# A two-layer streaming encoder on eight cores: when the last tile's norm is done, and where four modulation blocks are loaded

## The reference, cut to what matters

```python
def run_trunk(x, c, ...):
    for i in range(2):                     # layer 0: convolution module, layer 1: window attention
        mod = silu(c) @ w_mod[i] + b_mod[i]            # 6 * 2048 numbers for each sequence
        sh1, sc1, g1, sh2, sc2, g2 = split(mod, 6)
        h = rms_norm(x, norm_mix[i]) * (1 + sc1) + sh1
        y = conv_module(h) if i == 0 else attention(h)
        x = x + g1 * y
        h = rms_norm(x, norm_ffn[i]) * (1 + sc2) + sh2
        g, u = split(h @ w_gu[i], 2)                   # 2048 -> 2 * 5632
        x = x + g2 * ((silu(g) * u) @ w_down[i])       # 5632 -> 2048
    return rms_norm(x, norm_out), ...

def conv_module(h):                        # pw1: 2048 -> 4096, pw2: 2048 -> 2048
    a, gt = split(h @ w_pw1 + b_pw1, 2)
    z = depthwise_conv31(a * sigmoid(gt)) + b_dw
    return silu(layer_norm(z)) @ w_pw2 + b_pw2
```

## Time and profile before

| What | Value |
|---|---|
| Median of 3 runs | 3286.67 us |
| The profiled execution, its own time | 3290.7 us |
| Its span on the slowest core (core 1) | 3289.5 us |
| Spans of the eight cores | 3271.6 to 3289.5 us |
| PE busy | 3018.0 us, 92% |
| DVE busy | 1182.5 us, 36% |
| ACT busy | 674.9 us, 21% |
| POOL busy | 259.0 us, 8% |
| Granted clock of PE, mean over the core | 0.963 |

### The profile page before, as it was taken

The page is one execution under the profiler, slowest core; times in us unless marked ns, Lnnn a source line. Parts: engine busy times, 40 slices in busy tenths (PEclk is TensorE's granted clock), DMA queues, the critical chain, the costliest instruction groups (busy, mean ns, idle before and its releaser), DMA issues.

```text
span 3289.5 us, 55198 instructions; the slowest of 8 cores (3271.6 to 3289.5 us)
## 1 busy us (share of the span) xinstructions
PE 3018.0 (92%) x21834; PEld 1812.1 (55%) x21834; DVE 1182.5 (36%) x2585; ACT 674.9 (21%) x1413; POOL 259.0 (8%) x438
## 2 busy tenths in 40 slices
PE   1199998899899999999999889998999999999997
PEld 0055555445455555555555456666566666666664
DVE  0453335542143113141231749934222413131417
ACT  1132224332000000000001558833200000000012
POOL 0000001000000000000000113300000000000000
PEclk9599998999999999999999999989999999999999
DMA  9966766523767777777754222233243444444443
GB/s 193 195 114 123 140 130 139 131 52 71 135 128 124 134 128 128 129 128 126 126 95 65 43 58 60 55 59 71 52 77 58 84 77 78 71 71 77 78 73 111
DMA packets 78910, 327.74 MB, mean 100 GB/s; under 512 B 20849, under 2 KB 39921, under 8 KB 44465
## 3 DMA queue, kind: packets, MB, share of 16 engines
q0 software_dynamic: 41200, 283.66, 49.3%
q1 hardware_dynamic: 37458, 40.54, 4.2%
HBM read 593.07 MB, written 10.19 MB: 183 GB/s over the span
## 4 chain that ended last, share of the span: by engine, by line
PE 85%; DVE 6%; ACT 3%; DMA 2%; issue 2%; SPq 2%; another core or an unknown queue 1%; POOL 0%; DVEq 0%; ACTq 0%; POOLq 0%
PE ps L310 85%; SPq L305 2%; DVE SCR L316 1%; DMA X<-xT 1%; ACT SCR L313 1%; ACT HB L313 1%; DVE X L319 1%; DVE SCR L687 1%; DVE X L316 1%; DMA RING<-wgu 1%; DVE UBraw L1280 0%; POOL HB L699 0%; DMA kT_o<-UBraw 0%; ACT L313 0%
## 5 line engine op out<-in xcount | busy, mean ns | idle before, releaser
L310 PE MATMUL ps<-HB,RING 128*128 128x384 bf16 (+2 forms) x11712 | 1937.6, 326 | 71.0 <-ACT HB L313 22.2
L310 PEld LDWEIGHTS ps<-HB,RING 128*128 128x128 bf16 x11712 | 1142.3, 99 | 818.2 <-issue 122.0
L310 PE MATMUL ps<-UBraw,RING 128*128 128x384 bf16 (+3 forms) x5248 | 814.4, 313 | 1.9 <-ACT UBraw L313 0.7
L310 PEld LDWEIGHTS ps<-UBraw,RING 128*128 128x128 bf16 x5248 | 492.9, 98 | 302.0 <-issue 19.6
L319 DVE SCALAR_TENSOR_TENSOR X<-ps,MOD,X 128x16 f32<-128x16 f32 (+2 forms) x1120 | 453.9, 446 | 441.2 <-PE ps L310 438.4
L316 DVE TENSOR_TENSOR UBraw<-ps,SCR 128x384 bf16<-128x384 f32 (+2 forms) x264 | 144.2, 547 | 1188.3 <-PE ps L310 1182.1
L313 ACT ACTIVATE SCR<-ps 128x384 f32<-128x384 f32 (+4 forms) x314 | 155.5, 496 | 1785.2 <-PE ps L310 1762.6
L313 ACT ACTIVATE SCR<-X 128x384 bf16<-128x384 f32 (+3 forms) x224 | 135.8, 608 | 263.0 <-DVE X L319 260.6
L310 PE MATMUL ps<-SCR,ONESB 128*32 128x296 bf16 (+3 forms) x368 | 85.4, 336 | 87.1 <-ACT SCR L313 83.1
L128 POOL DMA_DIRECT2D RING<-wgu x88 | 46.8, 531 | 1172.7 <-PE ps L310 1172.6
L310 PE MATMUL ps<-RING,SCT 128*32 128x512 bf16 x768 | 60.5, 406 | 62.2 <-DMA RING<-wmod 35.1
(11 more groups left out here) (104 smaller groups left out, 1114.4 us busy)
## 6 DMA issues: line engine op xcount, KB each, us to landing
RING<-wmod POOLq DMA_DIRECT2D x96, 1024.0 KB, 14.1
RING<-wgu POOLq DMA_DIRECT2D x88, 1024.0 KB, 9.1
RING<-wdn POOLq DMA_DIRECT2D x40, 1024.0 KB, 9.4
RING<-wpw POOLq DMA_DIRECT2D x24, 1024.0 KB, 14.1
RING<-wqkv POOLq DMA_DIRECT2D x10, 1024.0 KB, 8.9
X<-xT SPq DMA_DIRECT2D x4, 2368.0 KB, 54.2
RING<-wo POOLq DMA_DIRECT2D x8, 1024.0 KB, 9.3
X<-xT SPq DMA_DIRECT2D x8, 768.0 KB, 4.5
```

What stands on the lines that cost most here:

```text
L310: return PE.emit(nc.tensor.matmul(out, lhsT=lhsT, rhs=rhs, start=start, stop=stop, **kw))
```

## The change

It has five parts. (1) Blocks 40 and 41 of layer 0's modulation move from `ffn` to pw2: they are planned after pw2_4 and pw2_5 and run in `proj_rest` behind the last item of these, in bank 7. The other six of that vector stay behind gu 2 to 7, also in bank 7. (2) In group 2 the modulation blocks between the four down blocks of group 1 are left out, and come later. (3) In pw1 the 24 blocks are dealt out to the chunks in another pattern, by which each vector ends with a chunk. (4) `norm_apply` has three buffers T1 instead of two and POOL takes c % 4 == 1; the sample columns of tile 2 are done between its first six chunks, in a work area of their own; `hb` holds a token for each chunk, and PE waits for chunk k ahead of its matmul k. SQ has seven buffers. (5) `proj_rest` flushes all squares at each item. The flush and finish of tile 2 move into a generator `last_tile`, which the next stage takes up: in `ffn` its first step comes between the gate and the up half of `gu(0,0)`, and six chunks each come ahead of the epilogues of `gu(0,1)` and `gu(1,0)`, the rest ahead of that of `gu(1,1)`; at k and v its first step comes behind the first `kv_group`.

```diff
@@ ffn_schedule @@
-    mods = [("mod", 0, 40 + b) for b in range(8)] if li == 0 else []
+    mods = [("mod", 0, 42 + b) for b in range(6)] if li == 0 else []
...
-    out += mods
-    mods = []
...
                 for b in range(4):
                     out.append(("dn", G - 1, b))
-                    if later:
+                    if later and G != 2:
                         out.append(later.pop(0))
@@ buffers @@
-        T1 = carve(SCR, 0, (128, 2, 416), F32)
-        SQ = [SQA[:, i, :] for i in range(4)] + [SQB[:, i, :] for i in range(4)]
+        T1 = carve(SCR, 0, (128, 3, 384), F32)
+        SQ = [SQA[:, i, :] for i in range(4)] + [SQB[:, i, :] for i in range(3)]
+        WS = carve(UBraw, 24000, (128, 2, KC, 16), F32)
@@ the plan of the ring @@
-            for _ in range(1 if c % 2 == 0 else 2):
+            for _ in range((2, 1, 2, 1, 2, 2, 1, 2, 1, 2, 2, 1, 1, 2, 1, 1)[c]):
...
             ring.add(f"pw2_{b}", wpw2[b], ALL)
+            if b in (4, 5):
+                ring.add(f"mod0_{36 + b}", wmod[36 + b], ALL)
@@ norm_apply @@
+            smp = sample_cols(nm) if t == 2 else iter(())
             for c in range(KC):
-                i = c % 2
+                i = c % 3
                 DVE.wait(t1free[i])
                 tt(cv3(T1[:, i, 0:n], lay, t), xv(c, lay, t, True), cv3(RSTD[:, t % 2, 0:n], lay, t), ALU.mult)
-                if c % 4 == 3:
+                tx = DVE.tick()
+                if c % 4 == 1:
...
-                yield
-            if t == 2:
-                DVE.wait(*t1free)
...
-            nm.hb[t] = (ACT.tick(), DVE.tick(), POOL.tick())
-            yield
+                nm.hb[t].append(t1free[i])
+                next(smp, None)
+                if c < KC - 1:
+                    yield
+            for _ in smp:
+                pass
+            nm.hb[t] = [(nm.smp, x) for x in nm.hb[t]]
+            rsfree[t % 2] = DVE.tick()
+            yield
+
+        def sample_cols(nm):
+            tk = [None, None]
+            for op in range(3):
+                for s in range(2):
+                    w = WS[:, s]
+                    DVE.wait(tk[s])
+                    if op == 0:
+                        tt(w, X[:, :, 1152 + 16 * s:1168 + 16 * s],
+                           RSTD[:, 0, 384 + 16 * s:400 + 16 * s].unsqueeze(1).to_broadcast([128, KC, 16]), ALU.mult)
+                    elif op == 1:
+                        tt(w, w, nm.A[:, :, 1 + s:2 + s].to_broadcast([128, KC, 16]), ALU.mult)
+                    else:
+                        tt(HB[:, :, 1184 + 16 * s:1200 + 16 * s], w, nm.SH[:, :, 1 + s:2 + s].to_broadcast([128, KC, 16]), ALU.add)
+                    tk[s] = nm.smp = DVE.tick()
+                    yield
+
+        def last_tile(nm):
+            norm_flush(nm, 0)
+            norm_finish(nm, 2)
+            yield
+            yield from nm.apply(nm, 2)
@@ proj_rest @@
-                norm_flush(nm, max(1, len(nm.pend) - 2))
+                if li == 0 and (b, h, t) in ((4, 1, 2), (5, 1, 2)):
+                    mod_block(0, 36 + b, 7)
+                norm_flush(nm, 0)
...
-                    norm_flush(nm, 0)
...
-            return gen
+            pump(gen, 40)
+            nm.war[2] = tp
+            return last_tile(nm)
@@ head of pw2, after each proj_group @@
+                norm_flush(nm1, len(nm1.pend) - 1)
@@ ffn @@
-                if j == 0:
-                    PE.wait(*nm_in.hb[t])
                 bank_wait(i)
                 for k in range(KC):
+                    if j == 0:
+                        PE.wait(*nm_in.hb[t][k])
                     mm(PS[i][:, 0:n], w[:, k, 0:128], hv(k, lay, t), k == 0, k == KC - 1)
                 tg = PE.tick()
+                if mid is not None:
+                    mid()
...
-            gu(0, 0, pm(6))
+            gu(0, 0, None, pm(1))
             gu(0, 1, pm(6))
-            gu(1, 0, pm(20))
-            gu(1, 1)
+            gu(1, 0, pm(6))
+            gu(1, 1, pm(40))
...
-                    mod_block(it[1], it[2], 4)
+                    mod_block(it[1], it[2], 4 if it[1] else 7)
...
-            norm_flush(nm, 0)
-            norm_finish(nm, 2)
-            return nm, nm.apply(nm, 2)
+            return nm, last_tile(nm)
@@ k and v @@
-            PE.wait(*nm2.hb[t])
             bank_wait(bi)
             for k in range(KC):
+                PE.wait(*nm2.hb[t][k])
...
-        pump(genN, 4)
         kv_group(0, 0, 0)
-        pump(genN, 4)
+        pump(genN, 2)
         kv_group(0, 1, 0)
-        pump(genN, 4)
+        pump(genN, 5)
         kv_group(1, 0, 0)
+        pump(genN, 5)
+        kv_group(1, 1, 0)
         pump(genN, 40)
-        kv_group(1, 1, 0)
```

More of the change, by code:

```diff
@@ L650, in __init__ @@
                 self.left = [KC] * 3
-                self.hb = [None] * 3
+                self.hb = [[] for _ in range(3)]
                 self.done = [None] * 3
+                self.smp = None
                 self.tok = None
                 self.war = [None] * 3
-        sqfree = [None] * 8
-        t1free = [None, None]
+        sqfree = [None] * 7
+        t1free = [None] * 3
         rsfree = [None, None]
@@ L662, in norm_sq @@
             n = CN[nm.lay][t]
-            i = nsq % 8
+            i = nsq % 7
             nsq += 1
@@ L702, in norm_apply @@
                 else:
-                    ACT.wait(DVE.tick())
+                    ACT.wait(tx)
                     act(hv(c, lay, t, True), cv3(T1[:, i, 0:n], lay, t), AF.Identity, scale=nm.A[:, c, 0:1], bias=nm.SH[:, c, 0:1])
                     t1free[i] = ACT.tick()
-                yield
-            if t == 2:
-                DVE.wait(*t1free)
-                for s in range(2):
-                    w = T1F[:, 256 * s:256 * s + 256].rearrange("p (c b) -> p c b", b=16)
-                    tt(w, X[:, :, 1152 + 16 * s:1168 + 16 * s],
-                       RSTD[:, 0, 384 + 16 * s:400 + 16 * s].unsqueeze(1).to_broadcast([128, KC, 16]), ALU.mult)
-                for s in range(2):
-                    w = T1F[:, 256 * s:256 * s + 256].rearrange("p (c b) -> p c b", b=16)
-                    sync(DVE)
-                    tt(w, w, nm.A[:, :, 1 + s:2 + s].to_broadcast([128, KC, 16]), ALU.mult)
-                for s in range(2):
-                    w = T1F[:, 256 * s:256 * s + 256].rearrange("p (c b) -> p c b", b=16)
-                    sync(DVE)
-                    tt(HB[:, :, 1184 + 16 * s:1200 + 16 * s], w, nm.SH[:, :, 1 + s:2 + s].to_broadcast([128, KC, 16]), ALU.add)
-                t1free[0] = t1free[1] = DVE.tick()
@@ L880, in build_nc @@
         nm1 = Norm(0, [5, 6, 4], A1, MOD[:, 0, 48:64, :])
+        nm1.apply = norm_apply
         HEADB = [0, 1, 2, 3, 4, 7]
@@ L991, in ffn @@
             pm = lambda k: (lambda: pump(gen_in, k))
-            gu(0, 0, pm(6))
+            gu(0, 0, None, pm(1))
             gu(0, 1, pm(6))
-            gu(1, 0, pm(20))
-            gu(1, 1)
-            assert nm_in.hb[2] is not None
+            gu(1, 0, pm(6))
+            gu(1, 1, pm(40))
             ring.release(f"gu{li}_0", gu(0, 2))
@@ L1227, in build_nc @@
         t_gb = make_g1b(1, "bo")
-        POOL.wait(t_gb, *nm2.hb[2])
+        POOL.wait(t_gb, *nm2.hb[2][KC - 1], *nm2.hb[2][KC - 2])
         def x_bias(c):
```

16 lines of the change are left out of this document (7 added, 9 removed).

## The result

| | before | after |
|---|---|---|
| median of the runs | 3286.84 us (4 runs) | 3250.28 us (4 runs) |
| lowest run | 3283.93 us | 3244.2 us |
| profiled execution | 3290.7 us | 3249.67 us |
| span of the profiled slowest core | 3289.5 us (core 1) | 3248.6 us (core 7) |

The ratio is 0.9884, with a 95% interval of 0.9869 to 0.9898. The change gains 1.2%, less than the 2% bound. The forecast was 3239 us, 11 us faster than what came; the range, 3222 to 3261, holds it.

A forecast was written before the change was run, and what follows sets the result against it. PE, busy 3018.0 of 3289.5 us, was taken as the bound, leaving idle and low-clock time to win. Loads 24.3 and seams 11.7, 11.0 and 1.2 sum to 48.2 off 3290.7, giving a median of 3239 us, range 3222 to 3261.

The forecast's parts named there:

- vector's end in pw1: In pw1, PE's wait for DVE's transposes at a vector's first block and the slow work behind it go: 6.5 us.
- group 0: At the end of group 0, PE's wait of 8.77 and the slow product behind it go: 10.1 us.
- group 2: Behind the half-size down blocks, PE's wait of 4.76 and the slow product behind it go: 7.7 us.
- seam behind pw2: From pw2 to ffn, gu(0,2) starts earlier with the norm's faster pace: gain 11.7 us, bounds 5 and 21.0.
- seam behind wo: From wo to ffn, the same chain with less cover on PE: gain 11.0 us, bounds 4 and 22.1.
- k and v: Seam to k and v: the wait for the last square goes, 3.7 us stay; gain 1.2, bounds -3 and 4.9.
- Rival C: A load is late elsewhere: pairs of full chunks in pw1 and pw2 miss, four waits of 4 us; 3255 us, chance 0.09.
- Rival A: At the seams, buffers don't help: the pace stays at 0.815 us a chunk; 3253 us, chance 0.12.
- the charge of 2.4 for clock: In the seam from pw2 to ffn, one product slowed behind a wait, 7.72 instead of 5.4: 2.4 us off the gain.
- Rival B: In the norm, DVE and POOL exclude each other: four chunks take 2.70, 2.3 us more a seam; 3244 us, chance 0.13.
- Rival D: No wait stays at the seams, which gain 21.0, 22.1 and 4.9 us: 3215 us, chance 0.07.
- Rival E: Slower: 144 waits by chunk inside accumulation groups cost PE 0.5 us each, +72 us; 3311 us, chance 0.05.

The follow-up runs named there:

- one behind chunk 0: The changed kernel with one modulation block of pw1 behind chunk 0 instead of two, each vector still ending with a chunk: 3238.36 us, ratio 0.9835.
- pattern alone: The kernel before with only the change's pattern of modulation blocks in pw1: 3298.31 us, ratio 1.0015.
- reverse experiments: Blocks 40 and 41 put back at the end of group 0: 3249.87 us; separately, modulation blocks put back between group 1's half-size down blocks: 3248.21 us.
- repeated run: The changed kernel itself, unaltered, run again on another chip: 3255.28 us, ratio 0.9882 to the kernel before.

## Why the prediction was right or wrong

| term | forecast | in the changed kernel | by itself |
|---|---|---|---|
| vector's end in pw1 | 6.5 | 3.6 | 6.2 (one behind chunk 0) |
| group 0 | 10.1 | with group 2: 15.7 | 12.2 less some 1.2 of the blocks |
| group 2 | 7.7 | | 5.4 |
| seam behind pw2 | 11.7 | 15.7 | |
| seam behind wo | 11.0 | 13.0 | |
| k and v | 1.2 | 1.2 | |
| first convolution | nothing | -10.0 on the mean, -16.7 on core 7 | -9.0 (pattern alone) |
| other stretches | nothing | 0.8 | |
| sum | 48.2 | 40.0 | |

**The time** was missed by 11 us because of one step: "each vector now ends with a chunk" was costed for the weight loads that a chunk of 22.1 us must cover (20.1, which holds: no load is late in pw1 on any core), and not for SP's copies that land behind them. Of the queues that the moved block meets I counted POOL's and left SP's out. The step cost 10.0 in the first stretch and another 2.4 in the next, whose convolutions then run partly at the lower clock; that is also why pw1 gave 3.6 and not 6.2. Rival C had the right kind (a transfer late in pw1, 3255) with the wrong object and place. The trace of before would have shown it: its copies behind chunk 0 land 12.9 to 14.7 us after issue with two loads beside them, and behind chunk 1, with three loads, 19.9 to 20.8; and the first convolution leaves only 15.7. That alone gives a wait of 4 to 5 us, the size of what three of the eight cores showed (3.1, 3.9 and 4.2).

**Luck.** That 11 us were missed and not some 15 is because errors cancelled: the seams gave 6.0 more than forecast, the loads only 2.1 less. And the range reached up to 3261 for rivals A and C, not for this wait.

**The loads.** Group 0 and group 2 together were forecast at 17.8; the reverse experiments give 12.2 and 5.4, 17.6 together, but 1.2 of that is the blocks' own time, which the move only puts elsewhere. Group 2 was mis-sized, because I took the rows of one core. Its wait and the slow product behind it, 4.76 and 2.9 on core 1, were 3.8 and 1.25 on the mean of the eight cores (a product of 17.44), 5.0 together for 7.7; with group 0 mended and group 2 as before they are 3.6 and 1.7. The same means for group 0 are 8.9 and 2.05, 10.9 together for 10.1. The stretch as a whole got 15.7 shorter, some 2 us less than the reverse experiments add up to; 0.9 of these lie in `gu(0,2)` and `gu(1,2)`, the first two products behind the seam (12.1 for 11.3), and come back with tile 2 flushed early or waited for whole. So the shorter seam hands part of its lateness on to the products behind it.

**The seams** were under-forecast by 4.0 and 2.0. The walk behind pw2 itself held almost to the instruction. With its times moved by the 7.3 us by which pw2 ends later here: reciprocal done at 748.3 (measured 748.28), gate half done at 735.0 (735.2), flush over at 738.9 (739.1), `gu(0,2)` at 761.2 (759.8). The walk's end was 1.4 too late, and the charge of 2.4 for clock stood on top of it. That charge is what failed most. Before, three products of the seam took 5.1 us more than at full clock (7.72, 6.74 and 12.22 for 5.4, 5.4 and 10.8); now 80 matmuls take 14.31 for 13.5 and the next 45 7.82 for 7.6: 1.0 in all. The wait for a bank was 1.19 instead of 2.5, and nothing stood ahead of `gu(1,0)`. The 2.5 held a slip: a product of 5.4 behind a wait of 1.0 from 740.5 on ends at 746.9 and not at 746.0, so the walk gives 1.6. I took the pace at 0.60; it was 2.51/4 = 0.63. What gave the 2.0 behind wo I did not look into.

**The parts of the seam**, each by taking it back: three buffers 4.0 and 4.0, samples between the chunks 4.0 and 2.2, waits by chunk 3.5 and 1.8, squares flushed at once 3.3 and 0.7, the place of tile 2's flush +1.3 and -1.4. They don't add: each is measured with the others there.

**Rival B** (DVE and POOL exclude each other) was put at 2.70 for four chunks; 2.51 was measured. But the exclusion is there. POOL's piece takes 0.70 alone, and 1.21 on the mean where two of DVE's products lie beside it (160 pieces on the eight cores). DVE is held too: of 400 of its products beside a piece of POOL, 9 of 50 on each core, 72 took 0.74 to 0.90, where none of the 624 others took more than 0.56. The Trainium skill, "SBUF — State Buffer", section "Who interferes with whom", has the second to issue blocked while the first runs. The trace agrees: the 72 products all began 0.26 us or more behind POOL's piece. What B had wrong is who pays: in the walk of tile 1 DVE keeps its 0.51 a product, and POOL's piece is the one that gets longer. It comes back to DVE as the wait for POOL's buffer, 0.47 in four chunks: 4 x 0.51 + 0.47 = 2.51. Taking POOL out changed the seams by 0.2 and 0.6 to the slower side, with ACT setting the pace instead, so it doesn't price this.

**Rival D** needed seams with no wait; waits of 2.9, 1.2 and 0.6 remain. **Rival E** is false: 16 matmuls behind 16 waits took 2.76 us, and 0.33 us a wait would have been needed. **Rival A** is false by the experiment with two buffers.

**Why 16 us and not 4.** Copies behind chunk 0 with three loads landed after 18 to 20 us on three cores of the profiled run, after 23.5 on one and after 29 to 32 on four; in the repeated run, after 18.2 to 19.0 on four cores and 28.8 to 30.3 on the other four. POOL issues chunk 1's two loads 17.5 us behind chunk 0's three (183.83 and 201.37 on core 7). The packets that the DMA engines moved show the rest. The loads are 128 packets of 8 KB each, and the copies, with one small transfer issued behind them, 720 packets of some 0.6 KB. While both wait, the packets go one for one: 542 of the loads and 556 of SP's between 191.5 and 215.5 on core 7. So the copies, which have more packets than three loads, are not done before the loads beside them are. When chunk 1's loads were issued, the three loads had moved 3.05 of their 3.15 MB on core 0, and 2.36 on core 7. These are the packets, MB and share of the engines in the 4 us after that issue, core 0 (193.21 to 197.21) first, then core 7 (201.37 to 205.37); q0 has the loads and q1 SP's transfers:

```profile
q0 software_dynamic: 68, 0.43, 83.5%
q1 hardware_dynamic: 407, 0.18, 16.4%
```

```profile
q0 software_dynamic: 82, 0.67, 94.5%
q1 hardware_dynamic: 82, 0.04, 5.2%
```

On core 0 the loads ran out and the copies finished; on core 7 the two further loads joined before that, and up to the landing of the copies 639 packets of loads went by, which is all five loads. On core 0 it was 398, little more than three.

What stays open is why the later cores are fed more slowly. In every pair of neighbours (0 and 1, 2 and 3, ...), in the profiled run, the repeated one and the one with the pattern alone, it was the core that began pw1 earlier, by its own time, that had the shorter wait. On core 7 the DMA engines moved 111 and 162 GB/s in the first two stretches of 8 us from 183.5, against 152 and 213 on core 0 from 175.4, both with their engines nearly full in the second. The Trainium skill, "HBM Reference", section "Specifications (TRN2)", says that the two cores of a domain share its bandwidth; the trace fits that, but no run here separates the cores of a pair, and none holds back chunk 1's loads.

## What to carry to other kernels

When a plan of loads is dealt out anew, list every transfer that is issued at the same moments, small ones on other queues too, and compare how late each lands with the compute that lies before its use; here the tightest place was the first of the pattern, where only one chunk of products lies ahead of the use and not a whole chunk. A seam is bounded by the engine with the longest chain, so walk it instruction by instruction; it came out right to 1.4 us here, and the edit that only moves work on PE, the place of tile 2's flush, won nothing. Read a wait on all cores before it is priced: the slowest core's 4.76 stood for a mean of 3.8. When several edits depend on a common token, take each back by itself, and also all together: samples and waits by chunk were worth 4.0 and 3.5 us each with the other there, and what they are worth together was not measured.

## What the hardware showed that I had not expected

- Four copies of 80 KB issued on SP land some 6 us later for one more load of 1 MB issued on POOL beside them: 12.9 to 14.7 us after issue with two loads, 18 to 21 with three, and 29 to 32 with three and two more that join in time. In the traces a packet of some 0.6 KB of the copies alternates with one of 8 KB of the loads, so it is the number of packets that counts, and 0.33 MB of copies last as long as 2 or 3 MB of loads.
- Cores in one kernel differ: the wait for these copies was 3.1 us on core 0, 7.8 on core 3 and 16.5 on core 7, and since the slowest core sets the time, the largest of them counts.
- After the 16.5 us of idle time the granted clock was 0.50, that is 1.2 GHz, in the first 3.6 us of the convolution, 0.89 in the next 3.1, and 1.00 (2.4 GHz) at the next convolution, for 2.1 us lost. The rows are busy times by engine, then clock, DMA share and GB/s:

```profile
217.90:221.50 3.60, 3.60 (x57) 2.50 (x61) 0.00 (x0) 0.66 (x2) 0.00 (x0) 0.50 0.34 95
221.50:224.60 3.10, 3.10 (x84) 2.31 (x76) 0.00 (x0) 1.32 (x4) 0.00 (x0) 0.89 0.00 0
242.60:247.20 4.60, 4.60 (x140) 3.48 (x132) 1.22 (x5) 1.98 (x6) 1.28 (x3) 1.00 0.84 132
```
